# Gaps between the k tiles of two stationary operands, and an offset between their high parts and rests

## The chip, the cores and the metric

The kernel runs on one core of one Trainium2 chip. The metric is the device time of one launch in microseconds, the median of 3 runs. A profiled execution of its own gave the rows below; its span goes from the first instruction to the last.

## The reference

Two layers of a decoder trunk on x of 256 rows and 1024 columns, float32. Each layer computes

```
h = rms_norm(x) * gain
proj = h @ w_in                                  # 1024 x 7428: inputs of four mixers, 4 x 1024 gate logits
y_n = mixer_n(proj) @ w_branch[rows of n]        # pooling, difference, stick-breaking, forgetting attention
x = x + (sum_n sigmoid(gate_n + b_n) * y_n) @ w_out
g, u = split(rms_norm(x) * gain @ w_ffn_up)      # 1024 x 5632
x = x + (silu(g) * u) @ w_ffn_down               # 2816 x 1024
```

## The kernel before

Each layer streams its weights in 144 units (`UNITS`); a unit is two k tiles of 128 rows by up to 512 columns. SyncE loads a unit into `raw` (6 slots), ScalarE rounds it into `w_hi` (L737), and VectorE writes what is left over into `w_lo` (L1013). Both are float32r tiles in rings of 5 slots. The activations are held turned, so that the contraction lies on the partitions, and are also split into a high part and a rest: `hT` for the normed input and later for the merged mixer output (8 k tiles of 256 columns), `oT` for the mixer outputs (10 k tiles), and `aT` for the activation between the two FFN products (22 k tiles).

For each k tile and each half t of the 256 rows, TensorE computes three products into the same PSUM bank: high part by `w_hi` (L1692), high part by `w_lo` (L1693), rest by `w_hi` (L1696). The 128 x 128 tile of `hT`, `oT` or `aT` is the stationary operand, loaded by a LDWEIGHTS ahead of every matmul, and 512 columns of `w_hi` or `w_lo` are the moving operand. The first item of layer 0 has its own form (L1720, L1726, L1739).

The order of the work is written out by hand: `MIXING_PE`, `MIXING_ACT` and `MIXING_DVE` say ahead of which unit each stage of the mixers (transposes, scores, softmax and so on) stands on each engine. The transposes for `hT` and `aT` go through PSUM; ScalarE copies the high part out (`norm_evac`, `merged_evac`, `act_evac`), and VectorE writes the rest (`lhs_rest`).

Of the 3162 matmul instructions at L1692, L1693 and L1696 that read `hT` or `aT`, 96 have 260 moving columns (item `pf`, 4 units in 2 layers) and the others 512; the first item adds 48 of 512. So 3114 matmuls with 512 moving columns read `hT` or `aT`: 2592 and 522.

Where the operands lie is set by the order in which `sb` is called. Tiles with `align=LINE` start at a multiple of 2048 bytes in each partition. In the built program `w_hi` starts at byte 43008, `w_lo` at 63488, `hT_hi` at 92160, `hT_lo` at 100352, `aT_hi` at 163840 and `aT_lo` at 186368, all of them multiples of 2048. A k tile of `hT` or `aT` takes 1024 bytes, and its half t starts 512 bytes in. So every stationary tile of these products starts at a multiple of 512 bytes, and every moving row at a multiple of 2048. A few other stationary tiles lie elsewhere: `sums` (L1532, the masks of the stick-breaking sums) starts at byte 151072, and the pool weights in `parameters` (L1508) at 158240, both 32 bytes past a multiple of 64; the constant that L1486 loads starts at byte 143360, a multiple of 512.

Of the kernel before, what the change touches and what calls it, by code (L numbers as in the profile page):

```python
# [25 lines left out]
F32R = mybir.dt.float32r  # L26
# [6 lines left out]
P = 128  # L33
TT = 2
SEQ = TT * P
DEPTH = 2
D = 1024
KD = D // P
# [3 lines left out]
KF = D_FF // P  # L42
# [3 lines left out]
LINE = 2048  # L46
# [263 lines left out]
def build(nc, x, attn_norm, ffn_norm, w_in, b_gate, w_branch, w_out, w_ffn_up, w_ffn_down, consts, params, turned_x, out):  # L310
# [8 lines left out]
    with ExitStack() as ctx:  # L319
        def sb(name, shape, dt=F32, stack=ctx, align=32):  # L320
            return stack.enter_context(nc.sbuf_tensor(name, shape, dt, align_bytes=align))

        event_order, more_in_first = {}, {}


# [24 lines left out]
        w_lo = sb("w_lo", [P, RING, 2, NC], F32R, align=LINE)  # L350

        x_sb = sb("x_sb", [P, TT, D])
        hT = [sb("hT_hi", [P, KD, SEQ], F32R, align=LINE), sb("hT_lo", [P, KD, SEQ], F32R, align=LINE)]
        wide = sb("wide", [P, TT, 4 * D])
        con = sb("con", [P, ncol])
        masks = sb("masks", [P, 3, P], BF16)
# [52 lines left out]
        probsT = sb("probsT", [P, 2, 384], F32, mixing)  # L409
        mixing.close()  # L410
        ffn_area = ExitStack()
        aT = [sb("aT_hi", [P, KF, SEQ], F32R, ffn_area, LINE), sb("aT_lo", [P, KF, SEQ], F32R, ffn_area, LINE)]
        ffn_area.close()


# [1428 lines left out]
```

How the kernel before makes its waits and increments, by code:

```python
        def wait_item(engine, layer, name, t):  # L527
            if t == 0 and name in EARLY:
                engine.wait_ge(early_done, nth(early_done, layer, name))
            else:
                engine.wait_ge(unit_done, nth(unit_done, layer, LAST[name]))
# [14 lines left out]
        @block.sync  # L547
# [3 lines left out]
            def load_unit(g):  # L551
                layer, u = divmod(g, U)
                n, k = UNITS[u]
                name, matrix, columns, _ = ITEMS[n]
                if g >= RAW:
                    sp.wait_ge(lo_ready, nth(lo_ready, *divmod(g - RAW, U)))
                rows = weights[matrix][layer, k * P:(k + 2) * P, :].rearrange("(k p) n -> p k n", p=P)
                at = 0
                for c0, w in columns:
                    sp.dma_start(raw[:, g % RAW, :, at:at + w], rows[:, :, c0:c0 + w]).then_inc(raw_loaded[g % RAW], 16)
                    at += w
                    filled[g % RAW] += 16
# [22 lines left out]
            for g in range(2, 4):  # L587
                load_turned_x(g)
                load_unit(g)
            load_unit(4)
            load_unit(5)
            sp.wait_ge(fills_ready, 1)
            for layer in range(DEPTH):
                for u in range(U):
                    if u in BIAS_AT:
                        g = BIAS_AT.index(u)
                        if g >= 2:
                            sp.wait_ge(gate_ready, nth(gate_ready, layer, (g - 2, 1)))
                        elif layer:
                            sp.wait_ge(gate_ready, nth(gate_ready, layer - 1, (6 + g, 1)))
```

## Time and profile before

| | |
|---|---|
| median of 3 runs | 861.67 us (861.63 to 861.88) |
| span of the profiled execution | 859.8 us |
| TensorE matmul busy | 855.7 us, 4246 instructions |
| VectorE, ScalarE, GpSimd busy | 593.9, 446.0, 113.6 us |
| granted TensorE clock | 1.00 in every slice |

The profile gives no duration of the launch beside the span; the median of the runs stands 1.8 us above the span. A busy matmul lasts longer than the distance to the next one, since matmuls overlap in the array: what counts is the distance from one start to the next, called the pitch here. The timeline gives starts to 10 ns, so a pitch is read over several matmuls.

### The profile page before, as it was taken

How to read it: one execution, taken by the hardware profiler on the slowest of the kernel's cores; microseconds unless marked ns; L12 is line 12 of the kernel's file. 1: busy time of each engine (PE TensorE's matmuls, PEld its weight loads, DVE VectorE, ACT ScalarE, POOL GpSimd, SP SyncE). 2: the span in 40 equal slices, each digit the busy share in tenths (PEclk: the TensorE clock that was granted, in tenths of full speed). 3: DMA queues.
4: the chain of work that ended last, by engine and by line, in shares of the span. 5: the costliest groups of instructions: out<-in, count | busy, mean ns of one | idle time of the engine just before them, and what ended most of it. 6: DMA issues, size and time to landing. Idle time of an engine off the chain costs nothing.

```text
span 859.8 us, 11140 instructions
## 1 busy us (share of the span) xinstructions
PE 855.7 (100%) x4246; PEld 711.6 (83%) x4246; DVE 593.9 (69%) x850; ACT 446.0 (52%) x646; POOL 113.6 (13%) x89
## 2 busy tenths in 40 slices
PE   9999999999999999999999999999999999999998
PEld 7888888888888888888888888888888888888887
DVE  7896967768777665564479768768696765565543
ACT  7567654854454444443364674558443644444431
POOL 0750101005401000000005401010063000000000
PEclk9999999999999999999999999999999999999999
DMA  9846656475657666555566465665665576665641
GB/s 343 290 150 190 200 175 183 148 228 180 188 184 236 190 195 190 182 185 189 162 186 178 119 195 158 196 197 162 205 196 179 151 234 183 185 190 177 195 147 50
DMA packets 87815, 160.53 MB, mean 187 GB/s; under 512 B 7505, under 2 KB 14161, under 8 KB 87761
## 3 DMA queue, kind: packets, MB, share of 16 engines
q1 hardware_dynamic: 87328, 159.16, 58.8%
q8 instruction: 34, 0.56, 0.3%
q10 hardware_dynamic: 432, 0.66, 0.2%
q14 instruction: 21, 0.16, 0.0%
HBM read 158.74 MB, written 1.05 MB: 186 GB/s over the span
## 4 chain that ended last, share of the span: by engine, by line
PE 93%; DVE 3%; DMA 2%; ACT 1%; SPq 1%; issue 0%; ACTq 0%
PE bulk L1692 28%; PE bulk L1696 28%; PE bulk L1693 28%; DMA raw<-in_w_in_dram 2%; DVE w_lo L1013 2%; PE bankAB L1432 1%; PE bankAB L1634 1%; PE bankT L1587 0%; PE bankAB L1576 0%; ACT w_hi L737 0%; PE bankAB L1441 0%; PE bankAB L1532 0%; PE bankO L1545 0%; PE bankT L1634 0%; PE bankO L1634 0%
## 5 line engine op out<-in xcount | busy, mean ns | idle before, releaser
L1013 DVE TENSOR_TENSOR w_lo<-raw,w_hi 128x1024 fp32r<-128x1024 f32 (+1 forms) x288 | 362.3, 1272 | 156.5 <-ACT w_hi L737 152.9
L737 ACT ACTIVATE w_hi<-raw 128x1024 fp32r<-128x1024 f32 (+1 forms) x286 | 297.7, 1049 | 245.3 <-PE bulk L1696 240.8
L1692 PE MATMUL bulk<-w_hi,hT_hi 128*128 128x512 f32 (+1 forms) x880 | 344.1, 391 | 0.2 <-DVE w_lo L1013 0.2
L1693 PE MATMUL bulk<-w_lo,hT_hi 128*128 128x512 f32 (+1 forms) x880 | 339.2, 385 | 0.0
L1696 PE MATMUL bulk<-w_hi,hT_lo 128*128 128x512 f32 (+1 forms) x880 | 336.5, 386 | 0.0
L1692 PEld LDWEIGHTS bulk<-w_hi,hT_hi 128*128 128x128 f32 x880 | 165.3, 188 | 33.2 <-DVE w_lo L1013 0.7
L1696 PEld LDWEIGHTS bulk<-w_hi,hT_lo 128*128 128x128 f32 x880 | 165.0, 188 | 33.4
L1693 PEld LDWEIGHTS bulk<-w_lo,hT_hi 128*128 128x128 f32 x880 | 165.4, 188 | 31.7
L1692 PE MATMUL bulk<-w_hi,aT_hi 128*128 128x512 f32 x174 | 68.0, 391 | 0.0
L1696 PE MATMUL bulk<-w_hi,aT_lo 128*128 128x512 f32 x174 | 67.7, 389 | 0.0
L1693 PE MATMUL bulk<-w_lo,aT_hi 128*128 128x512 f32 x174 | 67.7, 389 | 0.0
L709 POOL TENSOR_TENSOR wide<-wide 128x512 f32<-128x512 f32 x24 | 44.2, 1861 | 118.8 <-DVE wide L1309 118.4
L675 POOL TENSOR_TENSOR wide<-wide,ropeA 128x512 f32<-128x512 f32 x8 | 12.9, 1612 | 203.0 <-DVE wide L1116 202.9
L1696 PEld LDWEIGHTS bulk<-w_hi,aT_lo 128*128 128x128 f32 x174 | 32.7, 188 | 6.8
L1693 PEld LDWEIGHTS bulk<-w_lo,aT_hi 128*128 128x128 f32 x174 | 32.7, 188 | 6.7
L1692 PEld LDWEIGHTS bulk<-w_hi,aT_hi 128*128 128x128 f32 x174 | 32.7, 188 | 6.7
L1692 PE MATMUL bulk<-w_hi,oT_hi 128*128 128x512 f32 x80 | 31.3, 391 | 0.0
L1696 PE MATMUL bulk<-w_hi,oT_lo 128*128 128x512 f32 x80 | 31.2, 389 | 0.0
L1693 PE MATMUL bulk<-w_lo,oT_hi 128*128 128x512 f32 x80 | 31.1, 389 | 0.0
L935 ACT ACTIVATE wide<-bulk,y_ffn 128x512 f32<-128x512 f32 (+1 forms) x24 | 14.3, 649 | 18.2 <-PE bulk L1696 16.0
L1299 DVE SCALAR_TENSOR_TENSOR wide<-bulk,y_attn,bias 128x512 f32<-128x512 f32 x32 | 22.5, 745 | 0.7 <-PE bulk L1696 0.7
L1323 DVE SCALAR_TENSOR_TENSOR wide<-bulk,y_ffn,wide 128x512 f32<-128x512 f32 (+1 forms) x24 | 15.8, 702 | 10.2 <-ACT wide L935 10.2
(259 smaller groups left out, 720.7 us busy)
## 6 DMA issues: line engine op xcount, KB each, us to landing
raw<-in_w_in_dram SPq DMA_DIRECT2D x110, 512.0 KB, 4.1
raw<-in_w_ffn_up_dram SPq DMA_DIRECT2D x80, 512.0 KB, 4.4
raw<-in_w_ffn_down_dram SPq DMA_DIRECT2D x44, 512.0 KB, 3.3
raw<-in_w_branch_dram SPq DMA_DIRECT2D x20, 512.0 KB, 4.2
raw<-in_w_out_dram SPq DMA_DIRECT2D x16, 512.0 KB, 3.4
bias<-in_b_gate_dram SPq DMA_DIRECT2D x16, 256.0 KB, 4.4
raw<-in_w_ffn_up_dram SPq DMA_DIRECT2D x16, 256.0 KB, 3.2
raw<-in_w_in_dram SPq DMA_DIRECT2D x10, 256.0 KB, 2.7
```

The costliest lines, as they stand in the source:

```text
L675: pool.tensor_tensor(ta, x, ropeA[:, i, t:t + 1, :].broadcast_to([P, 8, HD]), ALU.mult)
L709: ins = pool.tensor_tensor(m, m, wide[:, t, n * D + j * NC:n * D + (j + 1) * NC], ALU.add)
L737: act.activation(w_hi[:, g % RING, :, 0:width], raw[:, g % RAW, :, 0:width], ACT.Copy).then_inc(hi_ready, 1)
L935: act.activation(ff_tmp(t, p, width), item_bank(layer, ITEM_AT[item], t)[:, 0:width], ACT.Sigmoid, scale=y_ffn[:, t:t + 1]).then_inc(ff_si ...
L1013: vec.tensor_tensor(w_lo[:, g % RING, :, 0:width], raw[:, g % RAW, :, 0:width], w_hi[:, g % RING, :, 0:width].bitcast(F32), ALU.subtract). ...
L1299: vec.scalar_tensor_tensor(out=wide[:, t, g * NC:(g + 1) * NC], in0=item_bank(layer, ITEM_AT[("gate", g)], t), scalar=y_attn[:, t:t + 1], ...
L1323: vec.scalar_tensor_tensor(out=s, in0=item_bank(layer, ITEM_AT[item], t)[:, 0:width], scalar=y_ffn[:, t:t + 1], in1=s, op0=ALU.mult, op1=A ...
L1432: ins = pe.matmul(dst, a[a_part], b[b_part], start=start and a_part + b_part == 0, stop=stop and a_part == 1, skip_group_check=True)
L1634: ins = pe.transpose(bank[name][:, k * P:(k + 1) * P], ff_act(t, p, blocks * P)[:, k * P:(k + 1) * P], identity)
L1692: pe.matmul(dst, hi, whi, start=(k == ks[0]), stop=False)
L1693: pe.matmul(dst, hi, wlo, start=False, stop=False)
L1696: ins = pe.matmul(dst, lo, whi, start=False, stop=(k == ks[-1] or g == DEPTH * U - 2 and i == 1 and t == 1))
```

## The change

`hT` and `aT` each become one tile that holds both parts. Each k tile of 256 columns is followed by `step` unused elements, and the rest starts `between` elements after the padded high part.

```diff
+        def staggered(name, blocks, step, between, stack):
+
+            size = blocks * (SEQ + step)
+            whole = sb(name, [P, 2 * size + between], F32R, stack, LINE)
+            return [whole[:, at:at + size].rearrange("p (k q) -> p k q", k=blocks)[:, :, 0:SEQ] for at in (0, size + between)]
...
-        hT = [sb("hT_hi", [P, KD, SEQ], F32R, align=LINE), sb("hT_lo", [P, KD, SEQ], F32R, align=LINE)]
+        hT = staggered("hT", KD, 16, 8, ctx)
...
-        aT = [sb("aT_hi", [P, KF, SEQ], F32R, ffn_area, LINE), sb("aT_lo", [P, KF, SEQ], F32R, ffn_area, LINE)]
+        aT = staggered("aT", KF, 4, 1, ffn_area)
```

For `hT` a k tile now begins every 1088 bytes, and the rest begins 8736 bytes after the high part: k tile k of the high part starts 64k bytes past a multiple of 1024, that of the rest 64k + 544 bytes past one (32 past a multiple of 64). For `aT` the distance is 1040 bytes and the rest begins 22884 bytes after the high part: 16k bytes past a multiple of 1024, and for the rest 16k + 356, which is 4 bytes past a multiple of 16. The moving operands, `oT`, `queries` and `keys` stay where they were. The tiles from `wide` to `fg` move up by 1056 bytes; `sums` and `parameters` are then at multiples of 64.

On all five engines the instructions, their shapes and their order are the same as before, with `hT` and `aT` in place of `hT_hi`, `hT_lo`, `aT_hi` and `aT_lo`. No semaphore and no DMA is added or removed.

## Rows read from the trace of the kernel before

**Rows 1.** The page: busy time by engine, the granted clock, the chain's shares
```profile
PE 855.7 (100%) x4246; PEld 711.6 (83%) x4246; DVE 593.9 (69%) x850; ACT 446.0 (52%) x646; POOL 113.6 (13%) x89
...
PEclk9999999999999999999999999999999999999999
...
PE 93%; DVE 3%; DMA 2%; ACT 1%; SPq 1%; issue 0%; ACTq 0%
```

**Rows 2.** Waits of TensorE: us in total, times, longest
```profile
PE bulk L1748 <- DVE warm L1358: 1.0, 1, 1.0
PE bulk L1720 <- ACT w_hi L973: 0.3, 1, 0.3
PE bulk L1692 <- DVE w_lo L1013: 0.2, 1, 0.2
```

**Rows 3.** Matmuls of the FFN: timeline with start us, duration us, engine, line
```profile
299.84 0.39 PE L1692 MATMUL bulk<-w_hi,hT_hi 128*128 128x512 f32 x1
300.07 0.39 PE L1693 MATMUL bulk<-w_lo,hT_hi 128*128 128x512 f32 x1
...
301.65 0.39 PE L1696 MATMUL bulk<-w_hi,hT_lo 128*128 128x512 f32 x1
301.88 0.39 PE L1692 MATMUL bulk<-w_hi,hT_hi 128*128 128x512 f32 x1
```

**Rows 4.** Weight loads under those matmuls, timeline
```profile
300.07 0.19 PEld L1696 LDWEIGHTS bulk<-w_hi,hT_lo 128*128 128x128 f32 x1
300.30 0.19 PEld L1692 LDWEIGHTS bulk<-w_hi,hT_hi 128*128 128x128 f32 x1
```

**Rows 5.** Matmuls after a mixer stage, timeline
```profile
47.13 0.50 PE L1692 MATMUL bulk<-w_hi,hT_hi 128*128 128x512 f32 x1
47.47 0.40 PE L1693 MATMUL bulk<-w_lo,hT_hi 128*128 128x512 f32 x1
47.70 0.40 PE L1696 MATMUL bulk<-w_hi,hT_lo 128*128 128x512 f32 x1
...
49.78 0.39 PE L1696 MATMUL bulk<-w_hi,hT_lo 128*128 128x512 f32 x1
50.01 0.39 PE L1692 MATMUL bulk<-w_hi,hT_hi 128*128 128x512 f32 x1
```

**Rows 6.** Matmul durations of L1693 by operand: ns min/median/max
```profile
L1693 PE MATMUL bulk<-w_lo,aT_hi x174: 387/389/396, 370.8 to 855.0; 128*128 128x512 f32 x174
L1693 PE MATMUL bulk<-w_lo,oT_hi x80: 387/389/395, 193.9 to 647.3; 128*128 128x512 f32 x80
```

**Rows 7.** Timeline around the pool products, matmuls and loads
```profile
162.65 0.40 PE L1696 MATMUL bulk<-w_hi,hT_lo 128*128 128x512 f32 x1
162.88 1.03 PE L1508 MATMUL bankT<-fq_gained,parameters 128*128 128x256 f32 x4
...
162.65 0.86 PEld L1508 LDWEIGHTS bankT<-fq_gained,parameters 128*128 128x128 f32 x4
163.53 0.19 PEld L1692 LDWEIGHTS bulk<-w_hi,hT_hi 128*128 128x128 f32 x1
```

**Rows 8.** Timeline around the stick-breaking sums and the cumulated logs
```profile
57.94 0.40 PE L1696 MATMUL bulk<-w_hi,hT_lo 128*128 128x512 f32 x1
58.18 0.34 PE L1532 MATMUL bankAB<-softplus_hi,sums 128*128 128x384 f32 x1
58.35 0.22 PE L1533 MATMUL bankAB<-softplus_hi,sums 128*128 128x128 f32 x1
...
57.95 0.19 PEld L1532 LDWEIGHTS bankAB<-softplus_hi,sums 128*128 128x128 f32 x1
...
108.98 0.39 PE L1696 MATMUL bulk<-w_hi,hT_lo 128*128 128x512 f32 x1
109.21 0.28 PE L1486 MATMUL bankT<-fg,con 128*128 128x8 f32 x2
```

**Rows 9.** Stretches: busy us of each engine; mixers of layer 0 and 1, FFN of layer 0
```profile
47.00:175.00 128.00, 127.84 (x723) 106.87 (x722) 99.04 (x185) 80.72 (x148) 19.11 (x14) 1.00 0.58 178
250.00:430.00 180.00, 180.00 (x819) 149.38 (x818) 106.19 (x120) 81.66 (x95) 3.70 (x7) 1.00 0.60 189
430.00:605.00 175.00, 175.00 (x953) 146.21 (x952) 136.57 (x241) 108.66 (x190) 30.78 (x22) 1.00 0.58 176
```

## The prediction

> **What bounds the kernel now.** I read the page first: TensorE is busy for the whole span, at a granted clock that reads 9 or more in every slice, and it carries 93% of the chain [rows 1]. Then the waits: TensorE waited 1.5 us in all, at three places [rows 2]. So the time is the sum of the matmuls' pitches, and only a change of pitch, or a new wait, can move it. The third view is the timeline in a stretch without mixer stages. From 299.84 to 301.88 lie nine pitches, 2.04 us, so 0.2267 us each [rows 3], and the weight load of the next matmul begins within 10 ns of the start of the present one and lasts 0.19 us, so it lies wholly under it [rows 4]. The duration that the profile gives a matmul goes with its pitch: 389 ns is the median for `aT` and `oT`, with 387 and 396 as the ends [rows 6].
>
> Is 226.7 ns all that 512 moving columns need? The nearest row with a slower moving stream and the same kind of load under it is the pool product: four passes, each with 256 float32 columns, take 1.03 us with the last one's own length of 0.38 us in it, so three pitches are 0.65 us, 217 ns each [rows 7]. If those 256 columns go at half the rate of float32r, they occupy the array as long as 512 of the others, and then 226.7 - 217 = 9.7 ns of each large pitch is not the array's. That inference from the rate is mine; the row shows only the 217. What else differs between the two is the speed at which the moving stream passes through SBUF while the stationary tile is read.
>
> The pitch is also not a constant of the instruction. After a mixer stage the same matmuls, on the same kinds of addresses, run from 47.70 to 49.78 with nine pitches in 2.08 us, 231.1 ns each, and only then settle: 49.78 to 50.01 [rows 5]. Nothing but the relative timing of the reads differs there. So the excess of a pitch depends on how the two streams stand to each other, and 226.7 is the state into which they fall when all stationary tiles start at multiples of 512 bytes. The change alters exactly that.
>
> **The change part by part.**
> - 2592 matmuls of 512 columns on `hT` and 522 on `aT` get other stationary addresses: 3114 pitches. The trace of before has none of them at the new addresses, so this is the unknown cost, and it is bounded from both sides. From below: the whole 9.7 ns go, 3114 x 9.7 = 30.2 us less. From above: the pitch is that of the unsettled stretch, 231.1 for all, 3114 x 4.4 = 13.7 us more. The value I take: durations in rows 6 go 2 to 3 ns below the settled 389 now and then (387), so states with a shorter pitch exist; I take 224, 2.7 ns less, for all of them: 3114 x 2.7 = 8.4 us less. It is nearer to the settled row than to the far ends, and that is why I choose it.
> - The 96 matmuls of 260 columns: at half of that each, 0.1 us. The 240 on `oT` keep their addresses and their 389 [rows 6]: nothing.
> - Evacuations into `hT` and `aT` (ScalarE and VectorE) write the same number of elements with another distance between four blocks. In the mixers VectorE is busy 99.04 of 128 us and 136.57 of 175, in the FFN 106.19 of 180 [rows 9], and TensorE does not wait for it; ten per cent on these few copies would be covered. Nothing.
> - The tiles from `wide` to `fg` move by 1056 bytes. They are read by transposes and small products; 16 to 32 bytes of phase in a few dozen loads, under 0.1 us either way.
> - What is late next: if TensorE is 1% faster, the mixer stages' chains on VectorE and ScalarE have 1% less time between two TensorE stages. VectorE at 77 and 78% busy still follows, but some stages will be waited for; I give back 0.3 us.
>
> Sum against the profiled execution: 859.8 - 8.4 - 0.1 + 0.3 = 851.6 us of span. The runs' median stands 1.9 us above the span of before, so **853.5 us**.
>
> The Trainium skill has a rule that speaks against this. Its page "SBUF — State Buffer", section "Who interferes with whom", gives TensorE two independent read ports, one for the moving operand and one for LDWEIGHTS, and says "PE and ACT never wait on anyone". By that rule the layout of the stationary tiles changes nothing. The trace agrees as far as other engines go, since TensorE's durations are the same in all stretches that I read, but not that both reads are free of each other in time, if rows 5 are read as I do. The page "TensorE: Matmul & The Clock Gate", section "Back-to-back issue gap", gives N/2.4 + 2.5 ns, which is 215.8 ns for 512 columns as an estimate from that page; the trace has 226.7. By it the floor of the sum would be 3114 x 10.9 = 34 us less.
>
> **The rivals.**
> *Slower: the new phases are bad ones.* For: where a large matmul has a load under it whose tile starts 32 bytes past a multiple of 64, its pitch is long. At 57.94, with `sums` loaded, it is 0.24 us [rows 8], at 162.65, with the pool weights, 0.23 [rows 7], both with a duration of 0.40 where the settled ones have 0.39. With the constant at a multiple of 512 under it, 108.98 to 109.21, the duration stays 0.39 [rows 8]. The rests of `hT` get just this offset. Price: a third of the pitches, 1038 x about 8 ns = 8.3 us more, 870; if each step from high part to rest also throws the streams out of the settled state, all at 231.1, 13.7 us more, 875.4. Against: these are single loads after a settled stretch, where any change may cost once; a repeated pattern may settle elsewhere, and the 384-column product at 58.18, again with such a load under it, has a pitch of only 0.17 [rows 8]. It decides if the mean pitch on `hT` comes out above 226.7.
> *Much faster: the excess goes nearly whole.* The pitch comes to 217: 30.2 us less, and about 1 us given back in the mixers, 832.5. For: the pool product. Against: no matmul of 512 columns in the trace comes near it; the least duration is 387, 2 ns under the settled one [rows 6].
> *No change: the excess is the price of a load, not of its place.* Any load of 128 x 128 under a moving stream takes its share of the reads, wherever it starts; the settled pitch is the same 389 for `hT`, `aT` and `oT`, and for both halves t, 512 bytes apart [rows 3, 6]. Time 861.7, within 0.8. Against: rows 5 and 8, where the price differs. The rule of the skill page above would give the same time. That the 4-byte shift of `aT` alone costs something belongs to the slower case: 174 loads of rests at a few ns, about 1 us.
>
> **How the numbers follow.** A run of this kernel can be told from another by about 0.2%, 1.7 us. Chances: forecast 0.42; much faster 0.10; no change 0.12; slower 0.36. What a phase does is not known from a settled row, and so the two signs are close; I put the shorter pitch first because the settled state of now is one of equal phases for 3114 loads, and rows 5 to 7 show excesses on both sides of it. The likeliest case's own range is 843 to 860. The range for 8 in 10 reaches into both others: 836 (between the forecast and the case of 832.5) to 875 (the slower case with all pitches at 231.1). Faster 0.52, same 0.12, slower 0.36.
>
> **What would show it.** In the profile of the changed kernel, nine pitches in the FFN stretch on `hT` should take 2.02 us instead of 2.04, the settled duration should be 386 or 387, that on `oT` still 389, and TensorE's waits should stay below 2 us. A mean pitch on `hT` over 227 with durations of 395 and more at L1693 (under which the rest is loaded) means the slower case; 389 throughout means no change; under 220, the large gain. If `hT` and `aT` move in different directions, the two offsets act by different rules, and I am wrong in treating them as one term. I am also wrong if the pitches shorten and TensorE's waits take the gain back.

## The result, and the profile after

The changed kernel takes 877.67 us (877.48 to 878.00, 3 runs) against 861.67: 16.0 us more, ratio 1.0185 (1.0171 to 1.0199). It is slower, and 2.7 us above the predicted range of 836 to 875.

The page of the changed kernel, with the busy times, the granted clock and the shares of the chain, answers to [rows 1]:

```profile
span 876.2 us, 11140 instructions
...
PE 872.5 (100%) x4246; PEld 713.3 (81%) x4246; DVE 593.2 (68%) x850; ACT 446.5 (51%) x646; POOL 112.3 (13%) x89
...
PEclk9999999999999999999999999999999999999999
...
PE 100%; DVE 0%; issue 0%
```

The span grew by 16.4 us, and TensorE's busy time by 16.8 with the same 4246 matmuls at the same clock. VectorE and ScalarE have the work that they had. TensorE waits once, at the start (us in total, times, longest; to [rows 2]):

```profile
PE bulk L1754 <- DVE warm L1364: 1.0, 1, 1.0
```

So the loss is pitch. The FFN stretch on `hT`, timeline, to [rows 3]:

```profile
304.06 0.39 PE L1698 MATMUL bulk<-w_hi,hT 128*128 128x512 f32 x1
304.29 0.39 PE L1699 MATMUL bulk<-w_lo,hT 128*128 128x512 f32 x1
304.52 0.40 PE L1702 MATMUL bulk<-w_hi,hT 128*128 128x512 f32 x1
304.75 0.40 PE L1698 MATMUL bulk<-w_hi,hT 128*128 128x512 f32 x1
304.99 0.40 PE L1699 MATMUL bulk<-w_lo,hT 128*128 128x512 f32 x1
...
306.16 0.39 PE L1698 MATMUL bulk<-w_hi,hT 128*128 128x512 f32 x1
```

Nine pitches from 304.06 to 306.16 take 2.10 us, 233.3 ns each; they took 2.04 before [rows 3]. In [rows 5] the stream settled after ten matmuls; here the pitch stays long through the whole stretch. By product and operand, all matmuls with 512 moving columns (count, busy us, mean ns of one, idle before):

```profile
L1698 PE MATMUL bulk<-w_hi,hT 128*128 128x512 f32 x848 | 339.0, 400 | 0.0
L1699 PE MATMUL bulk<-w_lo,hT 128*128 128x512 f32 x848 | 335.2, 395 | 0.0
L1702 PE MATMUL bulk<-w_hi,hT 128*128 128x512 f32 x848 | 331.4, 395 | 0.0
L1699 PE MATMUL bulk<-w_lo,aT 128*128 128x512 f32 x174 | 68.6, 395 | 0.0
...
L1699 PE MATMUL bulk<-w_lo,oT_hi 128*128 128x512 f32 x80 | 31.1, 389 | 0.0
```

`oT`, which did not move, keeps its 389 ns [rows 6]; `hT` and `aT` have 395 at the product with `w_lo`. L1698 on `hT` reads higher than the others because the first matmul after each stage stands there and is long in both kernels.

From here on a pitch is the mean distance from one start in the trace (which has them to the nanosecond) to the next, over neighbouring matmuls with 512 moving columns, distances over 290 ns (restarts) left out. It went from 227.3 to 232.8 ns on `hT` (about 2485 pairs) and from 226.9 to 232.2 on `aT` (514 pairs). 2485 x 5.5 + 514 x 5.3 = 16.4 us: as much as the span grew.

### The profile page after: what moved, and what is told of

Same layout as the page of the kernel before. It is cut to its first block, busy times and chain, and to the rows that moved or that the text cites. A ratio compares the mean times of both kernels' runs of the same rounds, so it can differ in the third digit from the quotient of the medians.

```text
span 876.2 us, 11140 instructions
## 1 busy us (share of the span) xinstructions
PE 872.5 (100%) x4246; PEld 713.3 (81%) x4246; DVE 593.2 (68%) x850; ACT 446.5 (51%) x646; POOL 112.3 (13%) x89
## 4 chain that ended last, share of the span: by engine, by line
PE 100%; DVE 0%; issue 0%
PE bulk L1698 30%; PE bulk L1699 30%; PE bulk L1702 30%; PE bankAB L1438 2%; PE bulk L1754 1%; PE bankAB L1640 1%; PE bulk L1726 0%; PE bankT L1593 0%; PE bankAB L1582 0%; PE bulk L1745 0%; PE bulk L1732 0%; PE bankAB L1538 0%; PE bankAB L1447 0%; PE bankO L1551 0%; PE bankO L1640 0%; PE bankT L1640 0%
## 5 line engine op out<-in xcount | busy, mean ns | idle before, releaser
L1698 PE MATMUL bulk<-w_hi,hT 128*128 128x512 f32 (+1 forms) x880 | 348.4, 396 | 0.0
L1699 PE MATMUL bulk<-w_lo,hT 128*128 128x512 f32 (+1 forms) x880 | 344.3, 391 | 0.0
L1702 PE MATMUL bulk<-w_hi,hT 128*128 128x512 f32 (+1 forms) x880 | 340.5, 391 | 0.0
L1698 PEld LDWEIGHTS bulk<-w_hi,hT 128*128 128x128 f32 x880 | 165.3, 188 | 37.5 <-DVE w_lo L1019 0.3
L1702 PEld LDWEIGHTS bulk<-w_hi,hT 128*128 128x128 f32 x880 | 165.0, 188 | 37.4
L1699 PEld LDWEIGHTS bulk<-w_lo,hT 128*128 128x128 f32 x880 | 165.8, 188 | 35.7
L1698 PE MATMUL bulk<-w_hi,aT 128*128 128x512 f32 x174 | 68.9, 396 | 0.0
L1699 PE MATMUL bulk<-w_lo,aT 128*128 128x512 f32 x174 | 68.6, 395 | 0.0
L1702 PE MATMUL bulk<-w_hi,aT 128*128 128x512 f32 x174 | 68.6, 394 | 0.0
L1702 PEld LDWEIGHTS bulk<-w_hi,aT 128*128 128x128 f32 x174 | 32.7, 188 | 7.7
L1698 PEld LDWEIGHTS bulk<-w_hi,aT 128*128 128x128 f32 x174 | 32.7, 188 | 7.6
L1699 PEld LDWEIGHTS bulk<-w_lo,aT 128*128 128x128 f32 x174 | 32.7, 188 | 7.6
L1698 PE MATMUL bulk<-w_hi,oT_hi 128*128 128x512 f32 x80 | 31.3, 391 | 0.0
L941 ACT ACTIVATE wide<-bulk,y_ffn 128x512 f32<-128x512 f32 (+1 forms) x24 | 14.4, 650 | 18.8 <-PE bulk L1702 16.8
L1329 DVE SCALAR_TENSOR_TENSOR wide<-bulk,y_ffn,wide 128x512 f32<-128x512 f32 (+1 forms) x24 | 15.8, 702 | 11.0 <-ACT wide L941 11.0
```

The lines of the kernel that those rows point to most:

```text
L941: act.activation(ff_tmp(t, p, width), item_bank(layer, ITEM_AT[item], t)[:, 0:width], ACT.Sigmoid, scale=y_ffn[:, t:t + 1]).then_inc(ff_si ...
L1329: vec.scalar_tensor_tensor(out=s, in0=item_bank(layer, ITEM_AT[item], t)[:, 0:width], scalar=y_ffn[:, t:t + 1], in1=s, op0=ALU.mult, op1=A ...
L1698: pe.matmul(dst, hi, whi, start=(k == ks[0]), stop=False)
L1699: pe.matmul(dst, hi, wlo, start=False, stop=False)
L1702: ins = pe.matmul(dst, lo, whi, start=False, stop=(k == ks[-1] or g == DEPTH * U - 2 and i == 1 and t == 1))
```

## The experiments

"Phase" is where a stationary tile starts, in bytes past a multiple of 256, relative to the moving row. In the kernel before it is 0 for every load of `hT`, `aT` and `oT`. The runs with a ratio were timed against the kernel before on the same chip; the three scans gave one time each and are read by their pitches alone. In all runs `staggered` has one argument more, `ahead`, the elements left unused in front (0 where the diff shows none). The diffs here leave out the lines that were replaced, and their comments are mine.

**Parts of the change.**

```diff
+hT = staggered("hT", KD, 16, 8, ctx)           # hT alone
```


> Only hT gets its gaps (64 bytes) and the shifted rest (32 bytes more); aT stays as before. Both theories: the loss of the change, 16.0 us, is a matter of pitches on hT and aT in proportion to their counts, so this alone costs 13 to 14 us (about 875), the pitch on hT is 232 to 233 ns, on aT and oT 226.7. If the two offsets act by different rules, the share is another.

```diff
+aT = staggered("aT", KF, 4, 1, ffn_area)       # aT alone
```


> Only aT gets its gaps (16 bytes) and the shifted rest (4 bytes more). Both theories: 2 to 3 us more than before (about 864), pitch on aT 232 ns, on hT 226.7.

```diff
+sb("moved", [P, 264])                          # ahead of wide; hT and aT as before
 wide = sb("wide", [P, TT, 4 * D])
```


> hT and aT as before; 1056 unused bytes stand ahead of wide, so that wide, con, sums, parameters and the small tiles move exactly as in the change. Both theories: nothing, 861.7 within 0.5. If the moved tiles carry part of the loss, it shows here.

`hT` alone: 874.98 us, 13.2 more (ratio 1.0153, 1.0138 to 1.0168), pitch on `hT` 232.8, on `aT` and `oT` 226.9. `aT` alone: 864.42, 2.6 more (1.0030, 1.0019 to 1.0042), pitch on `aT` 232.2, on `hT` 227.4. The moved tiles alone: 861.75 against 861.77 (1.0000, 0.9991 to 1.0009). The parts add up to 15.8 of 16.0 us, the tiles that only moved carry none of it, and the two offsets cost nearly the same per matmul (5.5 and 5.3 ns). Single loads did change in that last run, both ways: with `sums` at phase 64 instead of 32 the pitch of the large matmul above its load fell from 235 to 226 ns, and with the constant of L1486 at 32 instead of 0 it rose from 228 to between 233 and 235. They are too few to be seen in the time.

**Settling or place.** My theory of why the pitch was long was that the phase changes from load to load; the rival was that certain places are dear in themselves.

```diff
+hT = staggered("hT", KD, 0, 0, ctx, 8)         # all of hT at phase 32
+aT = staggered("aT", KF, 0, 0, ffn_area, 4)    # all of aT at phase 16
```


> No gaps: all of hT, high part and rest, starts 32 bytes later, all of aT 16 bytes later, so that every load of a tensor has one and the same phase, but not 0. Theory of settling (the pitch settles whenever each load stands to the moving rows as the last one did): 226.7 ns on both, 861.7 us. Theory of place (a load at 32 bytes past a multiple of 64 is itself dear): 235 ns on hT, 8 ns more for 2640 matmuls, 882 us or more.

876.53 us, 14.7 more (1.0171, 1.0156 to 1.0186). The matmuls with `w_lo` of that run (columns as above):

```profile
L1698 PE MATMUL bulk<-w_lo,hT 128*128 128x512 f32 x848 | 335.4, 395 | 0.0
L1698 PE MATMUL bulk<-w_lo,aT 128*128 128x512 f32 x174 | 67.9, 390 | 0.0
```

The phase of `hT` is one and the same in every load, and still the pitch is 233.2, near that of the changed kernel; `aT` at 16 has 227.6. Settling as I had put it falls: a constant phase is not enough, the place counts. My price for it, 235, was 2 ns too high. The stream does become regular here, but at a longer pitch: in the FFN stretches the pitches alternate between 231 or 232 and 235 ns, where at phase 0 they repeat 226, 227, 227.

```diff
+hT = staggered("hT", KD, 0, 0, ctx, 16)        # all of hT at 64
+aT = staggered("aT", KF, 0, 0, ffn_area, 64)   # all of aT at 256, that is 0
```


> As the run with constant phases, but hT 64 bytes and aT 256 bytes later, no gaps. Settling: 226.7 for both, 861.7 us. Place: any phase that is not a multiple of 512 has a price of its own, so the pitch on hT and that on aT come out away from 226.7, up or down, and tell whether a better place exists.

876.58 us (1.0173, 1.0158 to 1.0188). `hT` at 64: 233.3. `aT` at 256: 227.0, as at 0. So 64 is dear in a stream of such loads too, although the single load of `sums` at 64 above cost nothing, and 256 counts as 0.

**Gaps alone, shift alone.**

```diff
+hT = staggered("hT", KD, 16, 0, ctx)           # gaps, no shift
+aT = staggered("aT", KF, 4, 0, ffn_area)
```


> Gaps of 64 and 16 bytes, rests not shifted beyond them: the phase changes only from k tile to k tile. For hT the phases are 64k for both parts (8 x 1088 is a multiple of 512). Settling: the phase changes once in six matmuls, and it took 3 to 10 matmuls to settle after a mixer stage, so the pitch is still long, 230 to 233, 872 to 878 us. Place (32 past 64 is dear, 64 is not): hT at 226.7, only aT dearer, 862 to 865 us.

```diff
+hT = staggered("hT", KD, 0, 8, ctx)            # shift of the rests, no gaps
+aT = staggered("aT", KF, 0, 1, ffn_area)
```


> No gaps: only the rests are shifted, hT's by 32 bytes, aT's by 4. Settling: one load in three has another phase, so the stream is thrown out twice in three matmuls; pitch 230 to 233 for all three products, 873 to 878 us. Place: only the load of the rest is dear, 235 under L1693 (one in three), 226.7 at the other two, mean 229.5, 870 us.

Gaps alone: 874.73 us, 13.0 more (1.0152, 1.0135 to 1.0169), pitch 231.6 on `hT`, 232.0 on `aT`. Shift alone: 878.81 us, 17.0 more (1.0198, 1.0183 to 1.0213), pitch 233.0 and 233.3. The gaps alone cost 13.0 of the 16.0 us, the shift alone more than both together, so the two costs do not add. In the run with the shift alone the pitch differs by product. A stretch of its FFN, count, busy us and mean ns:

```profile
L1698 PE MATMUL bulk<-w_lo,hT 128*128 128x512 f32 x57 | 22.8, 400 | 0.0
L1697 PE MATMUL bulk<-w_hi,hT 128*128 128x512 f32 x56 | 22.2, 397 | 0.0
L1701 PE MATMUL bulk<-w_hi,hT 128*128 128x512 f32 x56 | 21.8, 389 | 0.0
```

The matmul with `w_lo` (L1698), under which the rest at phase 32 is loaded, has the longest pitch, 238.0 over the whole run, more than the 233.2 of the constant 32; the two others, with loads at phase 0 under them, have 232.3 (L1697) and 228.6 (L1701) instead of 227. So a step between a good and a bad place costs something on top, which place alone does not give (it expected 229.5 as the mean). On `aT`, whose rests stand at phase 4, the same order of loads gives 231.9 at L1698, 233.1 at L1697 and 234.9 at L1701: the mean is above the 232.4 of a constant 4, measured below, but the longest pitch is not over the load of the rest. Which of the three pays is therefore not settled by the place of the load under it alone.

**Steps between equal places.**

```diff
+hT = staggered("hT", KD, 0, 64, ctx)           # rest at 256
+aT = staggered("aT", KF, 64, 64, ffn_area)     # gaps of 256, rest 256 more
```


> hT: rest shifted by 256 bytes, no gaps; aT: gaps of 256 bytes and the rest 256 bytes more, so that all phases are multiples of 256 but change from load to load. 0, 256 and 512 each settled at 226.7 to 227.0 when constant. If a change of phase is what unsettles the stream: 231 to 234 on both, 875 to 879 us. If the place alone decides, and 256 counts as 0: 226.7 to 227 on both, 862 us.

861.82 us against 861.72 (1.0001, 0.9991 to 1.0010); 227.3 on `hT`, 226.9 on `aT`. The address steps from load to load, by 256 bytes, and nothing is lost. (The longer `aT` of this run lies over `forget_rows`, whose ones are written once at the start, so the forgetting attention of layer 1 computes something else; the instructions are the same.)

**Whose place counts.** All four large tiles of the products on `hT` start 32 bytes later, `oT` and `aT` stay:

```diff
+w_hi = sb("w_hi", [P, 8 + RING * 2 * NC], F32R, align=LINE)[:, 8:].rearrange("p (r i n) -> p r i n", r=RING, i=2)
+w_lo = sb("w_lo", [P, RING, 2, NC], F32R)
+hT = [sb("hT_hi", [P, KD, SEQ], F32R), sb("hT_lo", [P, KD, SEQ], F32R)]
```


> Moving tiles w_hi and w_lo and stationary hT all start 32 bytes later (no gaps); aT and oT stay at multiples of 512, so they now stand 32 bytes behind the moving rows. If the distance between moving and stationary addresses decides: hT at 226.7 (it was 233.2 with the moving tiles at 0), aT and oT at about 233, so 5 us more in all, 867. If the stationary address alone decides: hT 233.2, aT and oT 226.7, 876.5.

866.68 us, 5.0 more (1.0057, 1.0042 to 1.0072). The matmuls with `w_lo` of that run:

```profile
L1693 PE MATMUL bulk<-w_lo,hT_hi 128*128 128x512 f32 x848 | 330.2, 389 | 0.0
L1693 PE MATMUL bulk<-w_lo,aT_hi 128*128 128x512 f32 x174 | 68.7, 395 | 0.0
L1693 PE MATMUL bulk<-w_lo,oT_hi 128*128 128x512 f32 x80 | 31.6, 395 | 0.0
```

`hT` at byte 32 is back at 389 ns (pitch 227.4), because the moving rows moved with it; `aT` and `oT`, which kept the addresses that were good before, now have 233.3. (174 x 3 + 80 x 3) x 6.4 = 4.9 us, the loss of this run. It is the distance between the two addresses that decides, not either of them. The single load of `sums` agrees: it too moved from 32 to 64 here, but with the moving rows, and the pitch above it is still 235 ns.

**A better place?** Each scan gives each stretch of the program a constant phase of its own:

```diff
+h_parts = placed("hT", KD, {("attn", 0): 32, ("ffn", 0): 4, ("attn", 1): 12, ("ffn", 1): 24}, ctx)
+a_parts = placed("aT", KF, {0: 8, 1: 16}, ffn_area)     # elements; read as h_parts[which, layer]
```


> One constant phase for each stretch, no gaps. hT: 128 bytes in the mixers of layer 0, 16 in out and FFN of layer 0, 48 in the mixers of layer 1, 96 in out and FFN of layer 1; aT: 32 in layer 0, 64 in layer 1. If place decides with a period of 256 or less: 32, 64, 96, 128 and 48 at 231 to 234, 16 at 227.6 as aT had it; aT at 32 and 64 as hT at these, 233. If the tensor and not the phase decided, aT stays at 227.

> As the scan before, with hT at 4, 8, 192 and 384 bytes and aT at 128 and 4. If only the 16-byte piece counts, 4 and 8 act as 0 or as 16, 226.7 to 227.6. 384 is 128 more than 256: as 128. A phase under 226.7 would be a better place than that of the kernel before.

> Constant phases for hT again, those just below 256: 252 in the mixers of layer 0, 248 in out and FFN of layer 0, 240 in the mixers of layer 1, and 160 in out and FFN of layer 1; for aT the rest stands 256 bytes further, the high part at 0. The scans so far: 0 and 256 at 227, all others between 229 and 234. If 0 is the best place of a period of 256 bytes, all four phases of hT come out at 228 to 234; if the best place lies a little below 0, 252, 248 or 240 come out under 226.7, and the kernel could gain. aT: 226.9, since 0 and 256 are one place; 232 or more if the step from high part to rest alone unsettles it.

The mean pitches (ns), about 250 to 640 pairs for each phase of the scans, with the constant-phase runs above:

| phase | 0 | 4 | 8 | 16 | 32 | 48 | 64 | 96 | 128 | 160 | 192 | 224 | 240 | 248 | 252 |
|---|---|---|---|---|---|---|---|---|---|---|---|---|---|---|---|
| `hT` | 227.3 | 232.4 | 230.7 | 229.1 | 233.2 | 233.2 | 233.3 | 234.2 | 232.4 | 233.3 | 229.1 | | 227.9 | 233.3 | 231.0 |
| `aT` | 226.9 | 232.4 | | 227.6 | 233.3 | | 233.3 | | 232.4 | | | 233.3 | | | |

224 is from the run before, where the moving rows are 32 bytes ahead. `hT` at 384 has 232.4, as at 128, and `aT` with its rest at 256 has 227.0. Three rows of the scans, each in its stretch (the last two are 248 and 240 bytes), at the product with `w_lo`:

```profile
L1699 PE MATMUL bulk<-w_lo,hT 128*128 128x512 f32 x167 | 65.5, 392 | 0.0
```
```profile
L1700 PE MATMUL bulk<-w_lo,hT 128*128 128x512 f32 x164 | 64.9, 396 | 0.0
...
L1700 PE MATMUL bulk<-w_lo,hT 128*128 128x512 f32 x211 | 82.3, 390 | 0.0
```

The first is 16 bytes. The two tensors agree within half a nanosecond wherever both were tried, but at 16. No phase of the 15 is better than 0, 240 comes within a nanosecond, and a distance of 4 bytes costs 5 ns.

The means at 16, 240 and 252 hide something: there the same place has two levels. In the FFN of layer 0 of the first scan, `hT` is at 16 throughout, and its product with `w_lo` reads so from 280 to 299 us and from 303 to 322 us:

```profile
L1699 PE MATMUL bulk<-w_lo,hT 128*128 128x512 f32 x28 | 10.9, 389 | 0.0
...
L1699 PE MATMUL bulk<-w_lo,hT 128*128 128x512 f32 x28 | 11.0, 394 | 0.0
```

Of the five longest stretches between transposes there, three run at a pitch of 226.7 from start to end and two at 233.3. The two long stretches of `aT` at 16 run at 226.7 (and a short one at 233.4), which is why its mean is lower. At 252 a stretch of the mixers has 226.6 or 233.3, at 240 226.7 or 228.3. At 0 every stretch of 20 matmuls or more came to 226.7; at the phases from 32 to 224, at 4, 8 and 248, none did. So near 0 the place only allows the short pitch, and which level a stretch takes differs from restart to restart; what selects it was not tried.

The scans took 877.02, 873.85 and 871.45 us in one run each. There is no version here that beats the kernel before.

## Why the prediction was wrong

- **What bounds the kernel:** right. The whole change of time is a change of pitch on the loads that moved, and `oT` did not change.
- **The value taken for the unknown cost** is the step that failed: "I take 224, 2.7 ns less, for all of them". It measured 5.5 ns more on `hT` and 5.3 on `aT`. I argued from a settled duration of 389 with a minimum of 387 in [rows 6]. The starts in the trace show what a 387 is: on `aT` and on `oT` it is one matmul at L1693 with a pitch of 224 or 225, and it stands in nearly the same disturbed sequence as in [rows 5], where the pitches run 235, 233, 236, 224, 231, 236, 228, 233, 231 ns before they settle. So a pitch of 224 exists, but only once, behind one of 236, in a sequence whose mean is near 231; no stretch of the kernel before stays there. The least value of a distribution was used where only its mean can be had. Among the matmuls of 512 columns every deviation from the settled state that I had shown was costlier in the mean, and the forecast should have followed them.
- **The upper bound was too low.** 231.1 for all gave 13.7 us, 4.4 ns for each; measured were 5.5 and 5.3 ns, 16.0 us. The rows at a phase of 32 bytes [rows 7, 8] showed 0.23 and 0.24 us for one load, and these, at 3114 x 8, would have given 25 us and belonged in the range as its upper end. I used them for a third of the loads only.
- **The slower rival** had the right sign. Its place was half right: 32 bytes past a multiple of 64 is dear, but so is 64, and the period is 256 bytes, not 64. Its second half, "each step from high part to rest throws the streams out", is shown only for steps between unequal places. Its objection, that single loads after a settled stretch may not tell what a repeated pattern costs, was right: `sums` at 64 costs nothing alone, and 64 throughout costs 6 ns.
- **The much faster rival** has no run for it: no phase came under the pitch of before. Its row was also misread a little: the three pool pitches are 221, 215 and 215 ns, so the 217 is a mean with one longer pitch in it, and by 215 the bound would have been 11.7 ns for each, not 9.7. In the run that moved the pool weights by 1056 bytes they are 215, 215 and 216. What they owe to the slower stream was not tried, so no run shows that the 9.7 ns, or the 30.2 us made of them, could be had. The 215.8 ns that the prediction took from the Trainium skill ("TensorE: Matmul & The Clock Gate", "Back-to-back issue gap") is that section's figure for an isolated matmul, not for a stream with loads between, and the best pitch of 512 columns that lasts in any run here is 226.7.
- **No change** is refuted for the gaps given, and holds for gaps of 256 bytes. The sentence of the Trainium skill that I set against the change ("SBUF — State Buffer", "Who interferes with whom": two independent read ports, and TensorE never waits) does not agree with these runs, if it is taken as I took it, that the two reads of TensorE cannot delay each other: with nothing changed but the distance between the two addresses, the pitch goes from 227 to 233 ns.
- **The small terms:** evacuations, moved tiles and later waits were put at nothing, 0.1 and 0.3 us; the moved tiles measured nothing, TensorE's waits fell from 1.5 to 1.0 us, and the matmuls of 260 columns took 0.1 us more and not less. With a longer pitch there was nothing to give back.

What stays open is the mechanism inside. Shown: the cost depends on the stationary address relative to the moving one, on steps between unequal phases, and near phase 0 on something that differs from restart to restart. The period of 256 bytes rests on two pairs, 0 with 256 and 128 with 384, which have equal pitches. That the two reads meet in one part of SBUF is the reading I would give to it; no run here separates that from another cause with the same period. Also open is whether the 227 ns can be lowered at all at phase 0.

## What to carry to other kernels

In a stream like this one (float32r, 512 moving columns, a 128 x 128 load under each matmul), let the stationary tiles and the moving rows start at the same address modulo 256 bytes. Padding of 16 or 64 bytes between k tiles, harmless-looking and without a wait anywhere, lengthened the pitch by 1.9 to 2.2% here, and by 2.4% together with the shift of the rests. If padding is needed, take multiples of 256 bytes, and look at the pitch between starts, not at waits or busy shares, which showed nothing here. When a trace shows a settled value and short disturbances around it, price a change that disturbs by the mean of the disturbance, not by its best instant.

## What the runs showed of the hardware

- A stream of float32r matmuls with 512 moving columns and a 128 x 128 load under each runs at 226.7 to 227.3 ns when both operands start at the same place modulo 256 bytes, and at 229 to 234 in the mean at nearly every other distance that was tried, down to 4 bytes (232.4). At 16, 240 and 252 the same place gives 226.7 in some stretches and 228.3 (at 240) or 233.3 in others.
- Moving both operands by 32 bytes costs nothing (227.4); moving the stationary tiles alone or the moving rows alone costs 6 ns per matmul (233.2 on `hT` at 32; 233.3 on `aT` and `oT`).
- Steps between equal places (256 bytes) are free (227.3, 226.9). Between phases 0 and 32 in a pattern of three loads, the matmul over the load at 32 takes 238.0 and the others 232.3 and 228.6, though the loads under them stand at 0.
- At phase 0 the stream comes to its settled pitch after 0 to 16 further matmuls when another stage has stood between, most often after 2 or 9. The disturbed pitches are mostly an end piece of one sequence (235, 233, 236, 224, 231, 236, 228, 233, 231 ns).
- One load at a distance of 64 bytes under a settled stream cost nothing (226 ns); a stream of them runs at 233.3.
